# The sample's gated mixing run slot by slot beside the prompt's load stream, its merged channels kept in DRAM for a later output projection, and the FFN weights cast straight into SBUF

## The reference

```python
h = modulate(rmsnorm(x, g_pre_mix), sh1, sc1)
u_f, u_p, gate_logits = split(h @ w_in)          # 512, 512, 2048 columns
y_f = real(fft2(u_f over positions and group channels)) @ w_fo
y_p = pool_mix(u_p, w_pg, pool_scale) @ w_po     # centred means over 2, 4, 8, 16 positions
m = (sigmoid(g_f) * y_f + sigmoid(g_p) * y_p) @ w_out
x = x + gt1 * rmsnorm(m, g_post_mix)
h = modulate(rmsnorm(x, g_pre_ffn), sh2, sc2)
z = (silu(h @ w_gate) * (h @ w_up)) @ w_down     # d_ff = 2816
x = x + gt2 * rmsnorm(z, g_post_ffn)
```

## Time and profile before

| | |
|---|---|
| median of 3 runs | 2747.62 us (2742.37 to 2910.85) |
| the profiled execution | 2757.86 us |
| its span on the slowest core (core 2) | 2756.1 us |
| spans of the eight cores | 2728.9 to 2756.1 us |
| PE busy | 2466.7 us, 90% of the span |
| DVE, ACT, POOL busy | 898.0, 767.8, 804.5 us |
| DMA moved | 329.29 MB, 119 GB/s over the span |

### The profile page before, as it was taken

How to read it: one execution, slowest core, us unless ns; L and a number is a source line. 1 busy time by engine, 2 the same in 40 slices (tenths; PEclk the granted TensorE clock), 3 DMA queues, 4 the chain that set the end, 5 groups by cost and what they waited for, 6 DMA issues and landing times.

```text
span 2756.1 us, 37569 instructions; the slowest of 8 cores (2728.9 to 2756.1 us)
## 1 busy us (share of the span) xinstructions
PE 2466.7 (90%) x12028; PEld 1195.1 (43%) x12236; DVE 898.0 (33%) x1538; ACT 767.8 (28%) x1545; POOL 804.5 (29%) x723
## 2 busy tenths in 40 slices
PE   2594577888989998999989999999999999999997
PEld 1463343444444444444434444444444444444443
DVE  1774533344434444444221222212122122221221
ACT  2564623333333333333311111111111111111111
POOL 1111112367777776776411011010110100101001
PEclk9585788999999999999999999999999999999999
DMA  9799988597766655553762021120211202202011
GB/s 219 204 270 284 286 188 163 131 187 166 163 158 179 168 152 140 148 145 115 223 202 77 16 62 46 31 77 16 62 54 24 77 16 62 58 20 77 27 36 54
DMA packets 206691, 329.29 MB, mean 119 GB/s; under 512 B 125396, under 2 KB 134996, under 8 KB 204772
## 3 DMA queue, kind: packets, MB, share of 16 engines
q1 hardware_dynamic: 197748, 286.51, 36.1%
q0 software_dynamic: 8464, 38.28, 9.4%
q10 hardware_dynamic: 288, 2.10, 0.2%
HBM read 267.57 MB, written 86.52 MB: 128 GB/s over the span
## 4 chain that ended last, share of the span: by engine, by line
PE 78%; DMA 8%; POOL 5%; issue 4%; DVE 3%; SPq 1%; ACT 1%; POOLq 0%; DVEq 0%; ACTq 0%
PE p_b L350 78%; DMA s_a_xt_94<-xp 2%; DMA s_a_xt_94<-xs 2%; DMA s_a_xt_93<-xp 1%; SPq L129 1%; DMA s_ada_w_102<-w_ada 1%; DMA x_scr<-s_tmp_134 1%; DVE s_a_xn_96 L358 1%; POOL s_b_A_118 L366 1%; ACT s_a_xn_96 L354 1%; DMA s_a_xt_90<-xp 1%; DMA zf_scr<-s_a_Zf 1%; DMA s_a_T_65<-Tp 0%; POOL s_b_xn_124 L358 0%; POOL s_b_xn_123 L358 0%
## 5 line engine op out<-in xcount | busy, mean ns | idle before, releaser
L350 PE MATMUL p_b<-s_b_hT_115,s_b_wi 128*128 128x512 bf16 (+1 forms) x1152 | 234.1, 356 | 15.0 <-DVE s_b_gf_140 L366 5.4
L350 PE MATMUL p_b<-s_b_hT_146,s_b_wi 128*128 128x512 bf16 (+1 forms) x1152 | 235.9, 358 | 10.9 <-DVE s_b_hT_146 L358 5.8
L354 ACT ACTIVATE s_b_sa_218<-p_b 128x512 f32<-128x512 f32 x132 | 78.8, 597 | 365.7 <-PE p_b L350 362.8
L354 ACT ACTIVATE s_b_sa_217<-p_b 128x512 f32<-128x512 f32 x132 | 78.8, 597 | 348.9 <-PE p_b L350 348.9
L366 POOL TENSOR_TENSOR s_st_53<-s_st_53,s_half 128x1 f32<-128x1 f32 (+2 forms) x26 | 17.6, 677 | 526.8 <-DVE s_st_53 L369 486.1
L366 POOL TENSOR_TENSOR s_st_57<-s_st_57,s_half 128x1 f32<-128x1 f32 (+3 forms) x25 | 16.8, 672 | 520.2 <-DVE s_st_57 L369 476.4
L350 PEld LDWEIGHTS p_b<-s_b_hT_115,s_b_wi 128*128 128x128 bf16 x1152 | 111.8, 98 | 126.4 <-issue 23.5
L350 PEld LDWEIGHTS p_b<-s_b_hT_146,s_b_wi 128*128 128x128 bf16 x1152 | 113.2, 99 | 122.9 <-issue 13.6
L366 POOL TENSOR_TENSOR s_tmp_134<-s_tmp_134,s_xres_136 128x1024 f32<-128x1024 f32 x48 | 112.8, 2350 | 103.9 <-DVE s_tmp_134 L369 83.0
L366 POOL TENSOR_TENSOR s_tmp_135<-s_tmp_135,s_xres_137 128x1024 f32<-128x1024 f32 x48 | 112.8, 2350 | 85.9 <-DVE s_tmp_135 L369 77.0
L354 ACT ACTIVATE s_junk_138<-p_b 128x512 bf16<-128x512 f32 x96 | 56.7, 591 | 238.7 <-PE p_b L350 238.7
(11 more groups left out here) (479 smaller groups left out, 4922.5 us busy)
## 6 DMA issues: line engine op xcount, KB each, us to landing
s_xres_136<-xo SPq DMA_DIRECT2D x24, 512.0 KB, 4.3
s_xres_137<-xo SPq DMA_DIRECT2D x24, 512.0 KB, 5.9
x_scr<-s_tmp_134 SPq DMA_DIRECT2D x24, 512.0 KB, 4.3
x_scr<-s_tmp_135 SPq DMA_DIRECT2D x24, 512.0 KB, 3.0
s_xres_136<-x_scr SPq DMA_DIRECT2D x24, 512.0 KB, 4.2
y<-s_tmp_134 SPq DMA_DIRECT2D x24, 512.0 KB, 2.9
s_xres_137<-x_scr SPq DMA_DIRECT2D x24, 512.0 KB, 4.2
y<-s_tmp_135 SPq DMA_DIRECT2D x24, 512.0 KB, 3.1
```

Source lines behind the costliest of these rows:

```text
L350: S.op("pe", lambda e: e.matmul(out, lhsT=lhsT, rhs=rhs, start=start, stop=stop), reads=reads, writes=[bank], partial=True)
L354: S.op("act", lambda e: e.activation(out=out, in_=in_, func=func, **kw), reads=reads, writes=writes, partial=partial, full=full)
```

## The change

**Projection ahead of the second DFT.** Two steps of the first DFT go into a small buffer (`hxr`), and `project` multiplies them at once by `w_in`: 32 matmuls with the weights stationary and 264 (sample 272) columns moving. Only the projected `U` (33 groups x 512) is kept. `dft2` loses its projection and gets each group by a DMA transpose of [128, 1024] out of `U` (9 for the sample, 17 for the prompt). The stream's tiles are loaded two to a DMA of 1 MB; four such buffers hold two steps, as before. `squares` writes to a junk tile.

**B1 of the sample in the stream.** The sample's `dft2` ends at step 8; gate weights load from step 5 to 18; from step 13 each of the 23 remaining steps also does one block of a sample tile (`sample_pre`, `sample_main`, `sample_post`): the front end's transposes and loads, `b1_gc`, from block 4 on `b1_up`. With `gf`, `gp`, `up` and `win` in one buffer each. The remaining 9 blocks follow the stream, each with three steps of the prompt's `dft2`. `b1_wo` of the sample isn't done there: each block's merged channels [128, 512] go to DRAM (`mg_store`, 32 DMAs of 128 KB).

**Output projection of the sample later.** During the prompt's tiles (4 to 11) the 16 parts (`mg_load`, `b1_wo`, 16 matmuls each) stand in blocks 3, 5, 7 of tile 4 and in blocks 0 and 6 of the others. A prompt tile's own parts move from blocks 0 to 3 of the next tile to blocks 1 to 4. Scaling of front-end rows and of x2 goes from POOL to DVE.

**Conditioning.** `w_ada` comes in 48 blocks of 128 columns, 8 matmuls of 2 columns each, without transposes: 16 ahead of the stream, 8 after it, 24 in the prompt's tiles. The gate vector goes column by column to DRAM (`gate_store`, 2 x 1024 single floats) and comes back as rows.

**FFN weights.** No casts to DRAM; `gu_load` and the `dn` loads are POOL DMAs from f32 into SBUF, `gu` during the last B1 tile and the start of the FFN, `dn` behind them. The FFN takes tile 4 first (`SEQ2`).

```diff
-    tiles += [dft1([s1], [xp[s1, j] for j in range(4)], Eps, 4, Hxp, b_Hxp) for s1 in range(32)]
...
+    def project(pair):
...
+        for j in range(4):
+            ps, b_ps = banks.next()
+            for c in range(8):
+                mm(ps[:, 0:2 * ne], wfa[:, c, 128 * j:128 * j + 128], hv[:, c, :], c == 0, c == 7, [b_h, b_wfa], b_ps)
+            copy("act" if j % 2 else "dve", Uv[:, j, s1:s1 + 2],
...
+        def s0(g):
+            H, b_H = Hr.next()
...
+            S.dma("sp", H[:, 0:n, :], U[:, 2 * g:2 * g + n // 4].rearrange("p g j m -> p (g j m)"), reads=[b_U],
+                  writes=[b_H], transpose=True)
...
+    for t in range(NT):
...
+        run_late()
+        if t >= T0:
+            n, c = divmod(t - T0, 8)
+            sample_pre(n, c)
...
+        if s1 >= 0:
+            if s1 % 2 == 0 and s1 > 0:
+                project(8 + s1 // 2 - 1)
+            dft1(8 + s1 // 2, s1 % 2, tiles[t][3], [0, 1, 2, 3])
+        if t > 0:
+            squares(t + 2)
+        if t > 1:
+            norm(t + 1)
+            load(t + 3)
...
+        if t >= T0:
+            sample_main(n, c)
+        if 11 <= t < 19:
+            load_wi((2 * t - 18, 2 * t - 17))
+        if t >= T0:
+            sample_post(n, c)
...
+    for u, idx in enumerate(range(NT - T0, 32)):
+        n, c = divmod(idx, 8)
+        run_late()
+        sample_pre(n, c)
+        if todo:
+            todo.pop(0)()
+        sample_main(n, c)
+        for _ in range(2):
+            if todo:
+                todo.pop(0)()
...
+    def mg_store(n, c):
+        mg, b_m = mgs.pop((n, c))
+        S.dma("sp", mg_d[n, :, :, c, :].rearrange("s p x -> p s x"), mg[:].rearrange("p (s x) -> p s x", x=128),
+              reads=[b_m], writes=[b_mg[n]], partial=True)
...
     def gu_load(j):
-        S.dma("sp", gu[j][0][:].rearrange("p i k c -> p (i k c)"), gu_bf[j], reads=[b_gu[j]], writes=[gu[j][1]])
-
+        S.dma("pool", gu[j][0][:].rearrange("p i k c -> p (i k c)"), w_gu[j], writes=[gu[j][1]])
...
+            if n > 4 and 1 <= c < 5:
+                wo_at[8 * n + c] = (n - 1, c - 1)
+            elif parts and (c in (3, 5, 7) if n == 4 else c in (0, 6)):
+                wo_at[8 * n + c] = parts.pop(0)
...
+            if n == last:
+                if c == 1:
+                    b2_load(SEQ2[0])
+                    for j in range(10):
+                        gu_load(j)
+                if c == 4:
+                    b2_mod(SEQ2[0])
+                if c > 1:
+                    gu_load(8 + c)
```

898 lines of the change are left out of this document (514 added, 384 removed).

## The result

The changed kernel takes 2723.41 us in the median of four runs, beside 2745.12 us of the kernel before: a ratio of 0.9918, 95% interval 0.9893 to 0.9944. It is faster by 0.8%, less than the 2% that the forecast took for the least that tells, where 5.4% were forecast. All ratios leave out executions in which a die was in its slow state, here one of the kernel before, of 2910.85 us. The profiled run took 2723.73 us with a span of 2722.2 on its slowest core, core 5, which is 116 us over the 2606 of the sum. The 116 are 50 in T1 (666 instead of 616), 59 in tiles 4 to 11 (649 instead of 590) and 7 in the FFN (1407 instead of 1400).

A forecast was written before the change was run, and what follows sets the result against it. Prompt's stream bound by loads, B1 tiles and FFN keeping PE busy. T1 616 + tiles 590 + FFN 1400 = 2606 us span, 150 below 2756.1; 2747.6 - 150 gives 2598 measured, 8 in 10 for 2525 to 2695.

The forecast's parts named there:

- T1: Moment when tile 4, the first of the prompt, starts its first block: forecast 616 us against 796 before.
- (84 + 204) / 23 = 12.5: Steps with a sample block: 84 us for steps 13 to 18, 204 for steps 19 to 35 at 12 each.
- the case that I had priced at 12.8 in a rival: Stream step at a clock of 0.82 throughout, 12.8 us, named within the rival that the clock stays lower (chance 0.07).
- A longer chain in the step: Rival, chance 0.17: SP's in-order queue delays prompt loads; steps of 15 instead of 12 us, +96, total 2702.
- my signs of being wrong: Prompt loads over 15 us with PE waiting; clock 0.50 between 230 and 500; prompt tiles over 80 us; PE waiting for `gu`/`dn`.
- Steps 0 to 4, 95 us ("as now"): Start of the stream: 95 us, as now (97), since tiles first and weights behind them give and take little.
- Steps 5 to 12, 125 us from bytes and transposes: Stream steps: 32.8 MB is 113 us and 14 transposes 20; part of the weights may land later, so 125.
- The tail, 108 us: Blocks after the stream: PE 91 us, DMA 95 us; both bind, so 108.
- `gate_store` has one block before DVE needs the row: 0 to 15, I take 3: New stall in tiles 4 to 11: one block (8 us) before DVE needs the row; 3 us taken.
- Stalls 29.5 stay: Tiles 4 to 11: of 53.5 us of stalls before, 24.0 for `mg` go and 29.5 remain.
- Weight loads in tile 11, 8 us: POOL issues ten 1 MB loads in one block and waits from the ninth, other work queued behind: 0 to 15, 8 taken.
- FFN, 1404 - 9.7 + 6: FFN: the 9.68 us wait may go, f32 weight loads add 6: 1400 us, bounds -13 and +20.

The follow-up runs named there:

- the run with constants: Changed kernel with every reciprocal root on POOL in tiles 4 to 11 replaced by a constant that DVE writes: ratio 0.975 to the kernel before, 72.8 us a tile.
- the run that asks earlier: Changed kernel with DVE's scalings in tiles 4 to 11 placed later, behind other work, so roots are requested before they are needed: ratio 0.984, 75.9 us a tile.
- the combined runs: Changed kernel with six edits (0.975 to the kernel before), then also tile 5's front end and Z's first read earlier (0.970), then also the plain gate store (0.964).
- the last and fastest kernel: Changed kernel with six edits, the early front end and the plain gate store: 2647.76 us beside 2743.82 of the kernel before, ratio 0.964.

## Why the prediction was wrong

Right: that PE's free time in the stream can take the sample's blocks, and nearly its price. Steps 13 to 35 took 12.1 to 12.2 us each on six cores and 12.7 on two, where (84 + 204) / 23 = 12.5 were summed; an FFN tile took 114.00; the wait for `mg` at a tile's start went; the mean clock of the stream stayed far above its lower level (0.93 to 0.96 on the six cores from step 13 to step 35, 0.85 and 0.86 on cores 4 and 5). That the sum's 12.5 lies so near the slowest core's 12.7 is luck, though. I had built it from a chain of loads, with PE at 10.5 us and waiting for the rest. On cores 4 and 5 it was PE that filled the step, at 0.81 of full speed and busy for 147 to 148 of 150 us, the case that I had priced at 12.8 in a rival; on the others PE waited for less of a step than I had counted.

None of the rivals is what happened: the time is beyond "A longer chain in the step" (2702), and the hold of SP's queue that it rests on, priced at 96 us, cost some 18 by the run with plain copies. Of my signs of being wrong one came, a tile of the prompt over 80 us (tile 4, and tile 11 on the slowest core).

Wrong, by the terms of the sum, on the slowest core:

- *Steps 0 to 4, 95 us ("as now")*: 106.2. The gate vectors' load ahead of POOL's roots delayed PE's start to 41 us, but without it step 5 began only 2 us earlier. The term was copied from the kernel before, although the change reorders that stage's loads.
- *Steps 5 to 12, 125 us from bytes and transposes*: 142, and 146 in the median of the cores. I summed bytes and gave no time to the chain in which the first tile's front end, its pooled branch and the projection's copies follow one another through ACT and PE. Which link is worth what stays open.
- *The tail, 108 us*: with step 35 ending near 540, it was 126. The sum took PE and DMA each as a whole and had no term for two round trips: the conditioning weight behind the projection's loads (17.01 us) and the prompt's Z through DRAM (25.52 when the first was gone). They lie beside each other, so that removing one gave nothing. PE also waits 13.1 us there for the tables of the second DFT, another term that the sum lacks; no run took it away.
- *"`gate_store` has one block before DVE needs the row: 0 to 15, I take 3"*: 12, by the run with the plain store, near the upper end. I named the rule that spoke against it and gave it no weight. The Trainium skill (DMA: Bandwidth & Descriptors, Rules for kernel authors) says that a transfer whose last dimension isn't contiguous becomes one descriptor per element; the trace agrees, with 2160 packets of 4 bytes from 674.0 to 682.2 us for the 2048 elements of the two transfers, where the run with the plain store has 256 packets of 32 bytes. The runs add the price: the two landed after 10.5 us here and after 28.4 and 29.9 where other transfers stood beside them, against 1.9 in runs of 32 bytes. And the price isn't the store's landing alone: SP's queue and what stands behind it wait as well, from 674.06 to the row's load at 685.11 here.
- *"Stalls 29.5 stay" in the tiles, and the scalings moved to DVE "inside a load of 248 in 556 us"*: this is the largest failed step. Tiles 5 to 10 lose 8.2 us each, 6.2 of them to roots by the run with constants, 37 us in six tiles; 3.1 of the 6.2 are DVE's standing at them, by the run that asks earlier; of the rest it stays open. I asked whether DVE had room, and it had (40.8 of 78.3 us). But DVE asks for a root and uses it in its next instruction, and stood 0.8 to 3.8 us each time, and there are more of them a tile: six parts instead of four, and scalings that POOL did behind its own roots before.
- *Weight loads in tile 11, 8 us*: tile 11 lost 32 us on the slowest core and 21 in the median, 18 to 20 of the 21 by the combined runs (60 to 62 us). I priced POOL's queue alone: spreading its loads gave 11 us, of which 6 came back in the FFN. The four transposes of the first FFN tile, which the diff places in the same block, are another 6; on the slowest core they held SP's queue for 22.21 us. The second gate's store, ahead of this tile, had no term either, and tile 11 was 9 us shorter without it. These overlap: together they are more than the 21.
- *FFN, 1404 - 9.7 + 6*: 1407. The wait of the earlier trace rows went; one of 10.06 us came, from transposes that land late beside the weights. The bounds held it.

The small chance of the longer chain rested on "queues show no such stall in B1". That was so in the kernel before; the diff puts other transfers into these queues, and I priced them by their bytes and by their issue.

## What to carry to other kernels

Work moved into an engine's idle time can be priced from shares; the hand-overs at its borders can't. For each stage border list what is stored and read back, and for each in-order queue what stands behind every transfer that the change adds or moves. Where an engine waits for a small result of another, count the waits, not the busy time, and ask for the result an instruction group earlier. Look at the smallest transfers too: here 16 KB in four of them, written in runs instead of elements, were worth 18 us. And read a stage on every core that the trace holds before calling it unchanged: the slowest core of the changed kernel was an exception in the stream and in tile 11.

## What was not expected of the hardware

- Two element-wise transfers of 4 KB took 10.5 us to land on the slowest core of the changed kernel, and up to 18.2 on its others; in the runs that issue them beside other transfers they took 28.4 and 29.9 us on the slowest core. In runs of 32 bytes they took 1.9 us, and 9.2 in the last and fastest kernel.
- A DMA transpose of 128 rows took 1.2 us to issue at the least and up to 16.09 beside other transfers; four in a row held the queue for 6.4 to 10.9 us on seven cores and for 22.21 on the eighth. Replaced by plain copies in the stream and its tail, they were worth some 18 us of the whole, 7 of them in steps 5 to 12 and 6 in the tail.
- Cores 4 and 5 of the changed kernel were granted a clock of 0.81 in 320 to 470, with PE busy 98% of the time, while the two other cores of their die, at the same work, had 0.95 and 0.97. In the FFN all eight were granted 1.00 from 1430 to 2650 us, with PE busy all the time in the tile at 1500 to 1614.
